# The second layer's panels in another order: index queries, index keys, attention keys, values, attention queries

## What is computed

```python
q, k, v, q_idx, k_idx, w_idx = _split(h @ w_in, IN1_SIZES)   # 1024, 128, 128, 512, 64, 8 columns
x = x + g_m[:, None, :] * (dsa_mixer(q, k, v, q_idx, k_idx, w_idx) @ w_out)
```

## Time and profile before

| | |
|---|---|
| median of three runs | 2448.4 us |
| the profiled execution | 2447.52 us, span 2445.7 us |
| mean granted TensorE clock | 0.984 of full speed |
| busy | PE 97%, PEld 78%, DVE 55%, POOL 46%, ACT 39% |
| chain that ended last | PE 82%, DVE 8%, issue 3%, ACT, POOL and DMA 2% each |

### The profile page before, as it was taken

One profiled execution on the slowest core, in us unless ns is written; L12 is line 12 of the kernel. 1 busy time (PEld: TensorE's weight loads), 2 busy tenths in 40 slices (PEclk: granted clock), 3 DMA queues, 4 the chain that ended last, 5 costly groups with the idle time before them and its releaser, 6 DMA issues.

```text
span 2445.7 us, 34264 instructions
## 1 busy us (share of the span) xinstructions
PE 2377.0 (97%) x11797; PEld 1914.7 (78%) x11797; DVE 1346.3 (55%) x2195; ACT 952.6 (39%) x1556; POOL 1127.6 (46%) x529
## 2 busy tenths in 40 slices
PE   7999999999999999999999999999999999999998
PEld 6775778888877578888888678888888968888886
DVE  6777677673348843111147967364567474635455
ACT  3457433222335834222245453222246384322222
POOL 2436445545435543444455634434454463444433
PEclk9999999999999999999999999999999999999999
DMA  7640245554322022223222222323232201232222
GB/s 304 212 162 36 99 138 199 193 197 138 105 85 78 11 89 83 95 95 103 93 96 96 69 95 91 100 94 103 86 112 95 96 18 66 84 109 95 96 94 78
DMA packets 70098, 262.03 MB, mean 107 GB/s; under 512 B 7905, under 2 KB 8417, under 8 KB 68961
## 3 DMA queue, kind: packets, MB, share of 16 engines
q1 hardware_dynamic: 66816, 251.01, 30.0%
q10 hardware_dynamic: 3168, 9.50, 1.1%
HBM read 258.38 MB, written 2.10 MB: 107 GB/s over the span
## 4 chain that ended last, share of the span: by engine, by line
PE 82%; DVE 8%; issue 3%; DMA 2%; ACT 2%; POOL 2%; POOLq 1%; DVEq 1%; SPq 0%; ACTq 0%
PE bank L673 25%; PE bank L675 24%; PE bank L674 24%; PE bank L831 2%; PE bank L841 2%; PE bank L860 2%; DVE modraw L1876 1%; DVE acc L1602 1%; POOL w_lo L597 1%; DMA modraw<-in_blocks 1%; POOLq L661 1%; DVE bank L2210 1%; DVE x L1665 1%; DMA raw<-in_panels 1%; POOL prob L614 0%
## 5 line engine op out<-in xcount | busy, mean ns | idle before, releaser
L597 POOL TENSOR_TENSOR w_lo<-raw,w_hi 128x1024 fp32r<-128x1024 f32 x378 | 947.2, 2514 | 1185.3 <-ACT w_hi L1186 1183.4
L673 PE MATMUL bank<-h_hi,w_hi 128*128 128x512 f32 x1760 | 696.8, 396 | 14.6 <-DVE h_lo L1649 7.8
L674 PE MATMUL bank<-h_lo,w_hi 128*128 128x512 f32 x1760 | 690.2, 392 | 0.0
L675 PE MATMUL bank<-h_hi,w_lo 128*128 128x512 f32 x1760 | 689.7, 392 | 0.0
L1186 ACT ACTIVATE w_hi<-raw 128x1024 fp32r<-128x1024 f32 x378 | 392.5, 1051 | 414.3 <-PE bank L675 411.5
L673 PE MATMUL bank<-g_hi,w_hi 128*128 128x512 f32 x1072 | 421.6, 393 | 1.0 <-DVE g_lo L1686 1.0
L675 PE MATMUL bank<-g_hi,w_lo 128*128 128x512 f32 x1072 | 420.7, 392 | 0.0
L674 PE MATMUL bank<-g_lo,w_hi 128*128 128x512 f32 x1072 | 417.0, 389 | 0.0
L673 PEld LDWEIGHTS bank<-h_hi,w_hi 128*128 128x128 f32 x1760 | 333.9, 190 | 96.1 <-DVE h_lo L1649 8.7
L675 PEld LDWEIGHTS bank<-h_hi,w_lo 128*128 128x128 f32 x1760 | 333.7, 190 | 70.7
L674 PEld LDWEIGHTS bank<-h_lo,w_hi 128*128 128x128 f32 x1760 | 334.1, 190 | 69.3 <-issue 0.8
(11 more groups left out here) (295 smaller groups left out, 2510.7 us busy)
## 6 DMA issues: line engine op xcount, KB each, us to landing
raw<-in_panels SPq DMA_DIRECT2D x378, 512.0 KB, 3.5
modraw<-in_blocks SPq DMA_DIRECT2D x80, 512.0 KB, 4.9
first_mods<-in_first SPq DMA_DIRECT2D x4, 2048.0 KB, 21.9
x<-in_x SPq DMA_DIRECT2D x1, 2048.0 KB, 8.0
w<-in_w ACTq DMA_DIRECT2D x1, 2048.0 KB, 8.9
out<-yout ACTq DMA_DIRECT2D x8, 256.0 KB, 2.2
mask<-in_causal ACTq DMA_DIRECT2D x1, 1024.0 KB, 4.9
mask<-in_dilated ACTq DMA_DIRECT2D x1, 1024.0 KB, 6.9
```

The lines of the kernel that those rows point to most:

```text
L597: pool.tensor_tensor(w_lo[:, slot, :], raw[:, slot, :], w_hi[:, slot, :].bitcast(F32), ALU.subtract)\
L673: pe.matmul(out, w_h, m_h, start=start, stop=False)
L674: pe.matmul(out, w_h, m_l, start=False, stop=False)
L675: return pe.matmul(out, w_l, m_h, start=False, stop=stop)
```

## The change

The panel numbers of the layer get a new order, and the weights are laid out in memory to match: P_QI, P_KI, P_K1, P_V1, P_Q1. The first two index steps stand ahead of the value pair, the next two behind it. The attention keys are copied out by DVE and no longer by ACT. Since no panel now follows the last index step, the attention's waits are made explicit: the scores of pairs 0 and 1 wait for the relus that read banks 4 to 7, those of pair 2 for the last query panel's copy, and the score banks of the second attention are used in another order.

```diff
 P_QI = P_FFN0 + FFN_PANELS
-P_V1 = P_QI + 4
-P_KI = P_V1 + 2
-P_Q1 = P_KI + 1
-P_K1 = P_Q1 + KB
-P_OUT1 = P_K1 + 1
+P_KI = P_QI + 4
+P_K1 = P_KI + 1
+P_V1 = P_K1 + 1
+P_Q1 = P_V1 + 2
+P_OUT1 = P_Q1 + KB
...
-        SCORE_BANKS = ((0, 1, 6, 7), (0, 1, 6, 7), (6, 7, 0, 1))
+        SCORE_BANKS = ((0, 1, 6, 7), (6, 7, 0, 1), (6, 7, 0, 1))
...
+                    if run == 1 and n < 2:
+                        pe.wait_ge(relu_ready, 2 * (len(INDEX) - 1 + n))
+                    if run == 1 and n == 2:
+                        pe.wait_ge(bank_free, p_out)
...
-            token_panels(P_V1)
             panel(P_KI, P_KI % RING, h_hi, h_lo)
-
-            pe.wait_ge(bank_free, P_Q1)
+            panel(P_K1, P_K1 % RING, h_hi, h_lo)
...
-            for m in range(FIRST_INDEX):
+            pe.wait_ge(bank_free, P_K1)
+            for m in range(2):
+                index_scores(m)
+            token_panels(P_V1)
+            for m in range(2, FIRST_INDEX):
                 index_scores(m)
             for p in range(P_Q1, P_OUT1):
                 panel(p, p % RING, h_hi, h_lo)
-                if FIRST_INDEX + p - P_Q1 < len(INDEX):
-                    index_scores(FIRST_INDEX + p - P_Q1)
-            pe.wait_ge(bank_free, P_OUT1)
+                index_scores(FIRST_INDEX + p - P_Q1)
             attention(1, P_OUT1)
...
-            for p in range(P_QI, P_Q1):
+            for p in range(P_QI, P_V1):
                 split_hi(p + RING)
...
-            for n in range(IDX_HEADS):
+            for n in range(4):
+                index_relu(n)
+            for p in range(P_V1, P_Q1):
+                split_hi(p + RING)
+            for n in range(4, IDX_HEADS):
                 index_relu(n)
             for p in range(P_Q1, P_OUT1):
                 act.wait_ge(panel_done, p + 1)
-                act.activation(q1[:, p - P_Q1, :] if p < P_K1 else k1[:, :], bank[p % RING][:, :], ACT.Copy).then_inc(bank_free, 1)
+                if p == P_Q1:
+                    act.wait_ge(bank_free, P_Q1)
+                act.activation(q1[:, p - P_Q1, :], bank[p % RING][:, :], ACT.Copy).then_inc(bank_free, 1)
...
-            for p in range(P_QI, P_V1):
+            for p in range(P_QI, P_KI):
                 copy_out(p, qi[:, p - P_QI, :])
+            copy_out(P_KI, kiT[:, :])
+            copy_out(P_K1, k1[:, :])
             panel_ready(P_V1 + 1)
             for half in range(2):
...
-            copy_out(P_KI, kiT[:, :])
```

More of the change, by code:

```diff
@@ L2420, in laid_out @@
     index_weights[:, 0:IDX_HEADS] = w[:, 1856:1864]
-    parts += [panel_arrays(w[:, 1280:1792]), panel_arrays(w[:, 1152:1280]), panel_arrays(index_weights),
-              panel_arrays(np.concatenate([ki, ki], axis=1)),
-              panel_arrays(pairs(w[:, 0:1024], KB)), panel_arrays(w[:, 1024:1152]), panel_arrays(rows_by_pairs(f["l1_w_out"], KB))]
+    parts += [panel_arrays(w[:, 1280:1792]), panel_arrays(np.concatenate([ki, ki], axis=1)), panel_arrays(w[:, 1024:1152]),
+              panel_arrays(w[:, 1152:1280]), panel_arrays(index_weights),
+              panel_arrays(pairs(w[:, 0:1024], KB)), panel_arrays(rows_by_pairs(f["l1_w_out"], KB))]
     parts += ffn_panels(f["l1_ffn_wg"], f["l1_ffn_wu"], f["l1_ffn_wd"])
```

## The result

The changed kernel took 2453.7 us in the median of 14 runs (2447.86 to 2456.51), the kernel before 2448.47 (2445.1 to 2452.69). The ratio is 1.0019, 95% interval 1.0011 to 1.0026: 4.7 us slower, between 2.7 and 6.4. The forecast was 2455 us (range 2450 to 2459.5), with a chance of 0.57 for a change within 0.3%.

A forecast was written before the change was run, and what follows sets the result against it. PE, busy 97% of the span, bounds the kernel, with DVE's picks deciding when the attention starts. First mask +6.7 and clock +0.4 give +7.1 us on 2447.52, or 2454.6, stated as 2455 us (range 2450 to 2459.5).

The forecast's parts named there:

- PE's own work: PE's input panels: first query panel 4.6 us later, but PE through 1.1 us sooner, plus 0.69 for the key copy.
- DVE's chain decides: DVE's sums and picks ahead of the attention: late index weights start them later, putting the first mask 6.7 us later.
- The turns: Block 3's weighted sums on DVE alternate with POOL's subtractions, so picks begin 11.9 us later, at 751.9.
- The block of sums: DVE's eight weighted sums of block 3, forecast from 738.6 until the picks begin at 751.9.
- POOL's floor of +3.4: Attention start: POOL's additions lose their covering panel, first mask at least 3.4 us later; chance 0.14 that this decides.
- The clock, +0.4: PE behind its longer wait ahead of the transposes: low clock costs up to 1.3 us more, taken as 0.4.
- My price for the low clock before the change: Attention start before the change: 1.2 GHz for some 3.7 us after PE resumed, 1.8 us of work lost.
- The sum, +7.1: Whole kernel: +6.7 us for the later first mask and +0.4 for the clock, on 2447.52 us.
- The rivals: Attention start: POOL's floor +3.4, chance 0.14; sum 8 ahead +4.5, 0.18; costly clock +8 to +10, 0.15; faster, 0.03.
- Sum 8: DVE's last weighted sum of block 3: rival that it slips ahead of POOL's third subtraction, loss +4.5 us; chance 0.18.
- The costly clock (+8 to +10): Attention start: rival that a low clock goes on, ACT or DVE out of step in first pairs; 2456 to 2458, chance 0.15.

The follow-up runs named there:

- e1: Changed kernel with ACT's splits of the two weight panels behind the value pair moved behind the first query panel's copy; ratio 1.0008 to the kernel before.
- e11: The changed kernel once more, unaltered; ratio 1.0018 to the kernel before.
- e7: Changed kernel, value pair moved back, index steps one panel earlier, ACT copying attention keys, last query panel in PE's wait; ratio 0.9999 to kernel before.
- e9: e8 with the 16 rounds of picks left given one each to the attention's first 16 pairs; 2446.2 us, ratio 0.9988 to the kernel before.
- e8: e7 with 32 and not 33 rounds of DVE's picks ahead of the attention; ratio 0.9999 to the kernel before.
- e3: Changed kernel with e1's deferred splits and the index steps one panel earlier; ratio 1.0010 to the kernel before.

## Why the prediction was right

- **PE's own work.** The first query panel was forecast 4.6 us later; from the last copy of index queries it went from 22.06 (735.02 - 712.96) to 26.30 (733.26 - 706.96), 4.2 us. The 0.2 us for one more change between steps and panels are not seen in it. It was not on the path, as forecast.
- **DVE's chain decides.** Right, with each station within 0.8 us. The end of the value pair moved by 12.97 us (13.1 forecast), the first sum came at 25.57 (25.64), first mask to transposes was 4.94 again. What the forecast let drop out behind the picks (the waits for POOL and for scores, the held-up mask) did drop out.
- **The turns.** Right as a mechanism: e1 took the subtractions away and the sums were short again. The block of sums was mis-sized by 0.7: from its start to the first pick it took 12.6 us where I had 13.3. An instruction that was held up ends 0.54 to 0.55 us behind the one that held it (2.25 to 2.27 for a subtraction), and not its own 0.75 (2.35) later.
- **POOL's floor of +3.4.** Right: with the sums free it was 3.1, and the last pick waited for POOL.
- **The clock, +0.4.** From the transposes on, S - L, the changed kernel lost 0.28 us more than before, all of it up to the transposes of pair 2 (5.77 against 5.48); e11 lost 0.64. The size was right, in part by luck: the low stretch was 13.7 us and not 3.4, but only 4.1 of it lay where it costs. My price for the low clock before the change (1.8 us) was too high: 0.7 by the experiments.
- **The sum, +7.1.** The stage says +6.4 (e11: +6.8), 0.7 less, most of it the block of sums. The runs say +4.7, with an interval that just ends at 6.4. Behind the stage nothing is won back in the profile, so the difference between 4.7 and 6.4 is scatter between runs or something that one profile of each kernel does not show; it stays open. The clock's low stretch in the norm behind the attention differs between profiles (6.8 or 10.2 us), which can hide up to 1.7 us either way.
- **The rivals.** None came true in the changed kernel. Sum 8 did not slip ahead; the third subtraction took 2.59 and held it. The costly clock (+8 to +10) needed DVE or ACT out of step in the first pairs; the first pairs lost 0.3 us.

## What to carry to other kernels

When a step is moved later, look at what its consumers will then run beside: here the same eight sums cost nearly twice their time (12.5 and not 6.7 us) because POOL's subtractions had come to lie over them, and of the 11.1 us by which DVE's serial chain then started later, 6.1 reached PE; the waits that lay in that chain took up the rest. Two chains that end at one point are compared, not added, so a relief of the shorter one shows nothing until the longer is relieved. And a wait in front of a pipeline is a place for a panel of work that only later pairs need, if its copy and split are kept out of the first pairs' way (e7 to e9: 1.1 to 2.5 us in S; the runs show it for e9 alone).

## What the runs showed of the hardware

**The clock.** In the changed kernel, with PE idle from 787.3 on, the granted clock fell to 0.5 (1.2 GHz) at 789.4 and came back to 1.0 at 803.1, with PE busy for 2.5 us from 795.6 and again from 799.0 on. With extra matmuls of 6.28 us in that wait it fell 2.7 us after the last of them (PE had waited 1.89 us in between); with 7.99 us of them it fell 4.7 us after the last, behind waits of 0.19, 0.40 and 1.56 us. In e8, with PE's busy time at 1.0 to 2.0 us in each 2 us from 788 to 800, it did not fall. In the first pairs of the attention 3.4 to 4.9 us at 1.2 GHz cost 0.7 to 1.4 us, where DVE, ACT and POOL work beside PE.

**DVE and POOL.** A subtraction on POOL and sums with two inputs in SBUF on DVE alternate: over three sums and two subtractions neither went twice in a row, sums 2 and 3 taking 2.71 us instead of 0.75 and the subtractions 2.89 and 2.83 instead of 2.35. The picks are not held up: MAX8 takes 0.69 us at 748.35, in the middle of a subtraction (747.22, 2.41 us). But having one input is not what decides, for the mask has one too (`iacc`), and it took 1.89 us before, 1.50 in e1 and 1.91 in e3 beside a subtraction, and 0.36 in the changed kernel with none.
